# Sample rows of the input projection as fp32 products on 32-column tiles, and the stick-breaking sums of the prompt as rounded part and exact remainder

## The reference, cut to what matters

```python
def project(h, w_in, pos):
    B, T, _ = h.shape
    z = h @ w_in                       # h: 512 prompt rows, 8 sample rows; w_in: 1024 x 2840
    ...

def sb_attend(q, k, v, q_pos, k_pos):  # 8 heads of 64; for the prompt in blocks of 128 queries
    z = jnp.einsum('bqhd,bshd->bhqs', q, k) / math.sqrt(HEAD_DIM)
    mask = k_pos[None, :] < q_pos[:, None]
    log_1m = jnp.where(mask, jax.nn.log_sigmoid(-z), 0.0)
    after = lax.cumsum(log_1m, axis=3, reverse=True) - log_1m
    a = jnp.where(mask, jnp.exp(jax.nn.log_sigmoid(z) + after), 0.0)
    return jnp.einsum('bhqs,bshd->bqhd', a, v)
...
x = x + concat(rmsnorm(o_sb), rmsnorm(o_nsa)) @ w_out
x = x + square(relu(rmsnorm(x) @ w_up)) @ w_down
y = rmsnorm(x)
```

## Time and profile before

| | us |
|---|---|
| median of three runs | 1236.61 (1235.08 to 1242.04) |
| the profiled execution | 1237.38 |
| its span, first to last instruction | 1235.1 |
| PE busy | 1109.6 (90%) |
| PEld busy | 972.2 (79%) |
| DVE busy | 592.9 (48%) |
| ACT busy | 383.4 (31%) |
| POOL busy | 70.5 (6%) |

### The profile page before, as it was taken

One profiled execution on the slowest core, in us unless ns is written; L12 is line 12 of the kernel. 1 busy time (PEld: TensorE's weight loads), 2 busy tenths in 40 slices (PEclk: granted clock), 3 DMA queues, 4 the chain that ended last, 5 costly groups with the idle time before them and its releaser, 6 DMA issues.

```text
span 1235.1 us, 23204 instructions
## 1 busy us (share of the span) xinstructions
PE 1109.6 (90%) x8460; PEld 972.2 (79%) x8460; DVE 592.9 (48%) x991; ACT 383.4 (31%) x708; POOL 70.5 (6%) x83
## 2 busy tenths in 40 slices
PE   2999998789898997469999999999999999999993
PEld 2999898778788887335555566899999999998993
DVE  4221364667687863742134455544553234553332
ACT  4111212223333332126544455332222122231223
POOL 2000001111111100000000000010000000000002
PEclk9999998889899985559998999999999999999997
DMA  6428216999999932005567775222332322332221
GB/s 215 158 75 214 76 38 166 251 262 252 257 261 279 280 106 86 0 23 184 172 199 225 234 239 178 86 69 72 98 102 86 102 85 85 86 100 86 86 69 70
DMA packets 179085, 176.37 MB, mean 143 GB/s; under 512 B 13047, under 2 KB 139636, under 8 KB 176660
## 3 DMA queue, kind: packets, MB, share of 16 engines
q1 hardware_dynamic: 178610, 171.33, 49.2%
q10 hardware_dynamic: 418, 4.27, 1.1%
HBM read 169.67 MB, written 10.06 MB: 146 GB/s over the span
## 4 chain that ended last, share of the span: by engine, by line
PE 72%; SPq 10%; DVE 6%; issue 5%; DMA 4%; ACT 3%; POOL 0%; POOLq 0%; DVEq 0%; ACTq 0%
PE bank L605 67%; PE bank L609 5%; SPq L475 3%; SPq L514 3%; SPq L517 2%; DMA low_arena<-in_cache_nsa_slc_kv_dram 2%; SPq L468 1%; DMA high_arena<-in_state_nsa_win_kv_dram 1%; DMA high_arena<-in_x_sample_dram 1%; SPq L549 1%; ACT low_arena L1393 1%; SPq L544 0%; DMA high_arena<-in_w_in_dram 0%; DVE high_arena L1428 0%; POOL high_arena L1974 0%
## 5 line engine op out<-in xcount | busy, mean ns | idle before, releaser
L605 PE MATMUL bank<-high_arena 128*128 128x254 f32 (+8 forms) x1864 | 241.3, 346 | 8.8 <-ACT high_arena L1154 6.1
L605 PEld LDWEIGHTS bank<-high_arena 128*128 128x128 f32 (+4 forms) x1864 | 186.6, 153 | 49.6 <-issue 10.1
L609 PE MATMUL bank<-low_arena 128*128 128x128 f32 (+2 forms) x653 | 102.0, 299 | 36.1 <-DMA low_arena<-in_cache_nsa_slc_kv_dram 19.5
L1859 DVE TENSOR_TENSOR w_low<-high_arena,w_high 128x1024 fp32r<-128x1024 f32 x72 | 90.1, 1252 | 82.2 <-ACT w_high L1330 72.6
L605 PE MATMUL bank<-w_in_high,h_high 128*128 128x284 f32 (+1 forms) x400 | 119.2, 298 | 4.2 <-DVE low_arena L1482 2.6
L609 PEld LDWEIGHTS bank<-low_arena 128*128 128x128 f32 (+2 forms) x653 | 83.1, 159 | 47.4 <-issue 27.5
L605 PE MATMUL bank<-w_in_low,h_high 128*128 128x284 f32 (+1 forms) x400 | 118.6, 296 | 0.0
L605 PE MATMUL bank<-w_in_high,h_low_in 128*128 128x284 f32 (+1 forms) x400 | 118.5, 296 | 0.0
L1330 ACT ACTIVATE w_high<-high_arena 128x1024 fp32r<-128x1024 f32 x72 | 76.3, 1060 | 113.5 <-PE bank L605 112.5
L605 PE MATMUL bank<-a_high,w_high 128*128 128x256 f32 (+1 forms) x512 | 103.6, 283 | 5.3 <-issue 2.9
L605 PE MATMUL bank<-h_high,w_high 128*128 128x256 f32 (+1 forms) x512 | 103.7, 284 | 1.8 <-DVE h_low L1886 1.8
(11 more groups left out here) (205 smaller groups left out, 1540.4 us busy)
## 6 DMA issues: line engine op xcount, KB each, us to landing
low_arena<-in_cache_sb_kv_dram SPq DMA_DIRECT2D x128, 256.0 KB, 5.2
high_arena<-in_cache_sb_kv_dram SPq DMA_DIRECT2D x128, 256.0 KB, 3.6
high_arena<-in_cache_nsa_cmp_kv_dram SPq DMA_DIRECT2D x128, 128.0 KB, 5.5
high_arena<-in_w_up_dram SPq DMA_DIRECT2D x32, 512.0 KB, 4.0
high_arena<-in_w_down_dram SPq DMA_DIRECT2D x32, 512.0 KB, 3.7
high_arena<-in_w_in_dram SPq DMA_DIRECT2D x10, 1136.0 KB, 5.6
low_arena<-in_cache_nsa_slc_kv_dram SPq DMA_DIRECT2D x128, 64.0 KB
high_arena<-in_cache_nsa_slc_kv_dram SPq DMA_DIRECT2D x128, 64.0 KB, 3.0
```

The costliest lines, as they stand in the source:

```text
L605: return T.matmul(out, lhsT=l, rhs=r, start=start, stop=stop, **k)
L609: return T.transpose(out, in_, ident[0:n, 0:n])
L1859: V.tensor_tensor(w_lo_r[u], w_raw[u], w_hi[u], ALU.subtract).then_inc(sem(f"w_lo{u}"), 1)
```

## The change

It has two parts.

**Samples' projection.** The fifth row tile leaves the fp32r scheme. The samples' normed rows stay unsplit in a small tile `hs`, and for each block PE does 8 fp32 products (one for each k tile) with the raw `w_in` block as the moving operand and 8 columns of `hs` as the stationary one. Four of them go to column offsets 0, 32, 64, 96 of the array and bank rows 0, 32, 64, 96; the other four add to these. DVE then adds the four groups of 8 rows in a chain of one copy and three additions (`samples_out`). Since the remainder overwrites the raw block, the samples' products of block n+1 are done in the middle of block n, between row tiles 1 and 2, and `win_low(n+1)` waits for them. Block 0, whose remainder POOL writes early, is loaded a second time for them (`win_first`, from ACT's queue). The loops over blocks are written out.

**Stick-breaking sums.** DVE keeps the softplus values as rounded part (a copy) and remainder (a subtraction), and `sb_sum` multiplies each by `ntri` and `nones` (now rounded copies, made by two more ACT copies) as fp32r products. `sb_sum` moves in the step behind the samples' products and `sb_pv`.

```diff
             def z_rows(i, u, t):            # PE, row tiles 0 to 3: as before
+            def z_samples(raw):
+                for k in range(KD):
+                    c = 32 * (k % 4)
+                    ins = mm(bank[NT][c:c + B, 0:CB], hs[:, k, :], raw[:, k, :], k < 4, k >= 4, skip_group_check=True)
+                ins.then_inc(sem("z_mm"), 1)
+            def z_block(i, u, first=False, last=False):
+                pe.wait_ge(sem(f"w_lo{u}"), i + 1 + 1)
+                z_rows(i, u, 0)
+                if first:
+                    pe.wait_ge(sem("const_in"), 32)
+                    z_samples(win_first)
+                z_rows(i, u, 1)
+                if not last:
+                    pe.wait_ge(sem(f"win_in{1 - u}"), (i + u) * 16 + 16)
+                    pe.wait_ge(sem(f"z_ev{NT}"), i * 2 + (u + 2))
+                    z_samples(win[1 - u])
+                z_rows(i, u, 2)
+                z_rows(i, u, 3)
...
             def sb_sum(m):
-                pe.wait_ge(sem("sb_sp"), m + 1)
-                for h in range(2):
-                    ins = mm(out[:, 0:n], ntri, sp_tile(pr, i)[:, h], False, i == 3, skip_group_check=True)
-                    for j in range(3, i, -1):
-                        ins = mm(out[:, (j - i) * P:n], nones, sp_tile(pr, j)[:, h], False, j == i + 1, ...)
+                for low in range(2):
+                    pe.wait_ge(sem("sb_sp"), 2 * m + low + 1)
+                    for h in range(2):
+                        for j in range(i, NT):
+                            sp_ = (sp_low(pr, j) if low else sp_high(sums_hi_r, pr, j))[:, h]
+                            ...
+                            ins = mm(o, nones_r if j > i else ntri_r, sp_, False, low == 1 and j == NT - 1, ...)
...
-                if 1 <= s < SB_U + 1:
-                    sb_sum(s - 1)
                 for v in sample_steps(s):
                     sample_values(v)
...             # sb_pv(s - 2)
+                if 1 <= s < SB_U + 1:
+                    sb_sum(s - 1)
...
             win_high(0, 0)                  # ACT
+            act.dma_start(win_first, A["w_in"][0]...).then_inc(sem("const_in"), 16)
...
+            def win_low(n):                 # DVE
+                dve.wait_ge(sem(f"w_hi{n % 2}"), n // 2 + 1)
+                dve.wait_ge(sem("z_mm"), 5 * n - 1)
+                V.tensor_tensor(win_r[n % 2], win[n % 2], win_hi[n % 2], ALU.subtract).then_inc(sem(f"w_lo{n % 2}"), 1)
+            def z_block(n):
+                z_out(n, 0)
+                if n == 0:
+                    samples_out(0)
+                if n < NCB - 1:
+                    win_low(n + 1)
+                    samples_out(n + 1)
+                z_out(n, 2)
+                dve.wait_ge(sem("z_mm"), 5 * n + (5 if n == NCB - 1 else 6))
+                V.memset(st[0:1, 202:203], 0.0).then_inc(sem(f"win_free{n % 2}"), 1)
...
             def sb_soft(m):                 # DVE
-                V.scalar_tensor_tensor(out=sp_tile(pr, i), in0=bank_pair(...)..., op0=ALU.max, op1=ALU.add).then_inc(sem("sb_sp"), 1)
+                chain(V.scalar_tensor_tensor(out=v, in0=bank_pair(...)..., op0=ALU.max, op1=ALU.add))
+                V.tensor_copy(sp_high(sums_hi_r, pr, i), v).then_inc(sem("sb_sp"), 1)
+                V.tensor_tensor(low, v, high, ALU.subtract).then_inc(sem("sb_sp"), 1)
```

More of the change, by code:

```diff
@@ L293, in decoder_step @@
         win_hi, win_hi_r = zip(*(parts(f"w_in_high{u}", r.take(KD * CB), KD, CB) for u in range(2)))
+        win_first = view(r.take(KD * CB), KD, CB)
         r = Fields(r_at, TOTAL)
@@ L351, in decoder_step @@
         pbuf = view(late_at, 512)
-        spb = [z[:, NT, 0:2560].rearrange("p (h c) -> p h c", h=2), view(late_at, 2, 1280)]
+        z_r = rounded("z_parts", z_at, T5, COLS)
+        sums_hi_r = [z_r[:, NT, 0:2560].rearrange("p (h c) -> p h c", h=2), rounded("sums_high", late_at, 2, 1280)]
+        sums_hi = [s_.bitcast(F32) for s_ in sums_hi_r]
+        sums_lo_r = [[z_r[:, 0:2, O_QN:O_QN + 512], z_r[:, 2:4, O_QN:O_QN + 384], z_r[:, 0:2, O_C:O_C + 256], z_r[:, 2:4, O_C:O_C + P]],
+                     [rounded("sums_low0", osb_at + 4 * 512, 2, 512), rounded("sums_low1", osb_at + 6 * 512, 2, 384),
+                      z_r[:, 0:4, O_S:O_S + P].rearrange("p (h n) c -> p h n c", h=2), rounded("sums_low3", osb_at + 6 * 512 + 768, 2, P)]]
+        sums = view(r_at, 2, 512)
         w = Fields(late_at, TOTAL)
@@ L1099, in _ @@
             win_high(0, 0)
+            act.dma_start(win_first, A["w_in"][0].rearrange("(k p) c -> p k c", p=P)[:, :, (NCB - FIRST) * CB:(NCB - FIRST + 1) * CB]
+                          ).then_inc(sem("const_in"), 16)
             act.wait_ge(*signal("vcol_ev", 1))
@@ L1504, in rotary @@
                 dve.wait_ge(sem("rope_done"), t + 1)
[L1506 to L1517 removed]
+            for n in range(NCB):
+                if n >= FIRST:
+                    rotary(n - FIRST)
+                if n == NCB - 1:
                     rotary(NT)
[L1519 removed]
+                z_block(n)
             chain(V.memset(qbd[:, :, :], 0.0))
@@ L1766, in sb_soft @@
                     dve.wait_ge(sem("sb_c"), 4 * (pr - 1))
-                V.scalar_tensor_tensor(out=sp_tile(pr, i), in0=bank_pair(2 * (m % 3))[:, :, 0:n], scalar=0.0,
-                                       in1=ebuf[:, m % 2, :, 0:n], op0=ALU.max, op1=ALU.add).then_inc(sem("sb_sp"), 1)
+                v = sums[:, :, 0:n]
+                if m:
+                    dve.wait_ge(sem("sb_sp"), 2 * m)
+                chain(V.scalar_tensor_tensor(out=v, in0=bank_pair(2 * (m % 3))[:, :, 0:n], scalar=0.0,
+                                             in1=ebuf[:, m % 2, :, 0:n], op0=ALU.max, op1=ALU.add))
+                V.tensor_copy(sp_high(sums_hi_r, pr, i), v).then_inc(sem("sb_sp"), 1)
+                dve.wait_ge(sem("sb_sp"), 2 * m + 1)
+                low, high = sp_low(pr, i), sp_high(sums_hi, pr, i)
+                if len(low.shape) == 4:
+                    v, high = (a.rearrange("p h (n c) -> p h n c", c=P) for a in (v, high))
+                V.tensor_tensor(low, v, high, ALU.subtract).then_inc(sem("sb_sp"), 1)
             def sb_out(pr):
```

95 lines of the change are left out of this document (47 added, 48 removed).

## The result

| | before | after |
|---|---|---|
| median of the runs beside each other, us | 1239.32 (1235.08 to 1244.66, 4 runs) | 1223.21 (1222.58 to 1227.45, 4 runs) |
| ratio after / before | | 0.9875 [0.9826, 0.9924] |
| the profiled execution, its span, us | 1237.4, 1235.1 | 1223.6, 1221.7 |

What follows compares the result with a forecast made beforehand. PE was taken as the bound in both stages touched. Projection -13.7 and loop -12.8 us sum to -26.5: 1210.9 us for an execution like the profiled 1237.4, 1210.1 for the median, range 1200 to 1221.

Steps and rivals of the forecast that it cites:

- three new ones of 1.8: Attention loop: PE's present waits of about 1.4 us go, three new ones come: 0.1, 0.4 and 1.3 us.
- rival D: Loop: moved `sb_sum` uses up the one-step lag, each unit's chain runs bare, about 33 us a pair, 1273; chance 0.04.
- Rival A: Loop: each unit's remainder comes too late, DVE sets the pace, about 5 of 12.8 us left, 1218; chance 0.15.
- cancels: Projection: the clock falls after the late load's hole as it does now, 1.7 us, so no net cost.
- The products: Projection: 31.2 us of fifth-tile products go, samples' products at 1.08 us a block, 10.8 in all, come: -20.4 us.
- The late load: Projection, block 5: PE waits 8.1 us for block 6's `w_in` load where it waited 2.3, so +5.8 us.
- The margin of 0.4 us: Projection, other blocks: load there at 5.9 us, PE asks at 6.3; +1.0 us put for copies in flight and jitter.
- Sums, what goes and comes: Loop: fp32 sums of 9.25 us a pair become 5.6 as fp32r products, -14.6 us in four pairs.
- The small products, the disputed term: Loop sums: fp32r products of 128 columns take 0.066 to 0.14 us, 0.11 taken; the skill gives about 81 ns.
- Sums, the named waits: Loop: 1.3 us at the first NSA steps, +0.4 for mask copies on ACT, +1.0 for waits on pages.
- B: Projection: the late load does not hurt since the queue ahead runs faster; the 8.1 us vanish, 1202; chance 0.05.
- C: Projection: the four column offsets do not overlap, 3.9 us a block, total 1235, no change; chance 0.03.

Runs made afterwards that it cites:

- acc_first: Changed kernel with `acc_out` ahead of `sb_soft` in DVE's queue; 1213.43 us, 0.9821 of the kernel before, loop 76.5 us.
- acc_no_rest: `acc_first` without the remainder's products in `sb_sum` and PE's wait for them; 1204.69 us, 0.9732 of the kernel before, loop 68.7 us.
- queue_late: Changed kernel with compression weights and 16 cache loads issued behind all ten `w_in` loads; 1212.60 us, 0.9823 of the kernel before.
- proj_only: Changed projection with the sums of the kernel before; 1224.18 us, 0.9894 of the kernel before, loop 88.5 us.
- sum_first: Changed kernel with `sb_sum` back in its old place on PE, ahead of samples' products and `sb_pv`; 1219.96 us, 0.9881 of the kernel before.

## Why the prediction was wrong, step by step

**The step that failed** is "Following all 16 units in this way, I find the waits that PE has now ... gone, and three new ones of 1.8". What was followed were the units: scores, passes, softplus with its two new instructions, sums, values. The samples' work in between was counted as time that PE has to spend, and not as work that itself waits for DVE. `gather_values` waits for `acc_out`, and `acc_out` stands in DVE's queue behind the very instructions whose number the change raises. That wait takes 6.5 us in the loop, and the slow clock behind it 6.2, together 12.7 of the 13.9 us that `acc_first` brings back. In the prediction's sum the term "three new ones of 1.8" had to hold these 12.7 us and did not. With `acc_first`'s 9.8 us off, the median is 1213.4, inside the range.

The whole account, by the two profiles: the loop came out 14.7 us above its forecast (+1.9 against -12.8) and the projection 2.1 (-11.6 against -13.7). The unchanged stages came out 3.8 us below, which is luck. Together the span fell by 13.4 us instead of 26.5.

**The bound of a moved instruction.** The prediction weighed the move of `sb_sum` by the lag of its own unit (rival D) and by the cover of the remainder (rival A). It did not ask what `sb_sum` had been covering from its old place, and that was the gather, with 3.5 us to spare. Rival A gave 1218 for another reason; `acc_no_rest` shows that the remainder does not set the pace.

**The clock** was allowed for in the projection ("cancels") and not in the loop, since no hole was expected there. In the projection it nearly cancelled: the low clock cost 1.9 us behind the hole of 9.9 us (`queue_late`) and 1.7 behind the one of 2.3 us before. In the loop it cost 3.4 and 2.8 us, and no term held them.

**Projection, -13.7 forecast, -11.6 measured.** The products: a block of 13.84 us against 13.7, with 1.26 us for the samples against 1.08; in ten blocks 1.8 us too little. The extra time stands on both sides of the piece: its first product starts 0.22 us behind the last full one (67.33 to 67.55), and the second full product behind it 0.24 after the first (68.62 to 68.86), where full products start 0.13 apart. The Trainium skill (TensorEngine Tiling, Key Properties) says that changing the tiling mode drains the engine, and gives no time for it. The prediction's estimate for such a drain on the way in and on the way out, 1.08 + 0.13 = 1.21, is near the 1.26 measured; no run here separates the drain from the rest. The late load: its issue at 108.82 (forecast 108.2), the wait in block 5 behind tile 1, with tiles 2 and 3 hiding both parts, all as worked out. But it landed after 10.2 us instead of 8.1, so the wait was 9.9 and not 8.1. The load before landed while 216 GB/s were moved, this one at 192; why was not tested. The prediction took one landing from one trace as fixed: in the profiles with the changed projection and the old queue the same wait is 8.5 (`acc_first`), 9.9, 10.0 (`acc_no_rest`), 10.1 (`proj_only`) and 11.1 us (`sum_first`). The margin of 0.4 us in the other blocks held, so the 1.0 us put there for jitter was not needed. DVE's chain for the samples was as forecast, 1.9 us:

```profile
71.52 0.43 DVE L1534 COPY low_arena<-bank 8x284 f32<-8x284 f32 x1
71.99 0.92 DVE L1536 TENSOR_TENSOR low_arena<-low_arena,bank 8x284 f32<-8x284 f32 x2
72.94 0.45 DVE L1537 TENSOR_TENSOR low_arena<-low_arena,bank 8x284 f32<-8x284 f32 x1
```

**Sums, what goes and comes**: 9.25 us a pair became 6.14 and not 5.6, so the sums gave 12.4 us and not 14.6. The small products, the disputed term, were sized right:

```profile
558.14 0.28 PE L621 MATMUL bank<-sums_high,ntri_r 128*128 128x128 f32 x1
558.26 0.39 PE L621 MATMUL bank<-sums_low,ntri_r 128*128 128x128 f32 x2
```
```profile
543.24 0.33 PE L621 MATMUL bank<-z_parts,ntri_r 128*128 128x256 f32 x1
543.41 0.22 PE L621 MATMUL bank<-z_parts,nones_r 128*128 128x128 f32 x1
543.47 0.33 PE L621 MATMUL bank<-z_parts,ntri_r 128*128 128x256 f32 x1
```

Two products of 128 columns in a row start 0.12 us apart (558.14 to 558.26). A 256 with a 128 takes 0.23, from 543.24 to 543.47, which is the 0.12 + 0.11 that was taken; the starts inside the pair are 0.17 and 0.06 apart, so how the 0.23 divides is not shown. The Trainium skill (TensorE: Matmul & The Clock Gate, Back-to-back issue gap) has about 81 ns for the sustained product of 128 columns; the trace's 0.12 us doesn't agree, and the measurement decides. What was too small is the edge of each run of sums: the four sizes take 2.69, 1.79, 1.07 and 0.59 us by the timeline of `acc_first` (548.23 to 550.92, 542.73 to 544.52, 538.45 to 539.52, 535.73 to 536.32), each 0.15 to 0.19 over its products (four groups of 0.63, 0.40, 0.23 and 0.11), where 0.1 was allowed for all four together.

**Sums, the named waits**: 1.11 us at the first NSA steps (forecast 1.3), the mask copies 3.7 - 3.3 = 0.4 (0.4), waits for pages below 2 us (1.0). DVE's copy of 1024 elements took 0.69 (0.78), its subtraction 1.23 (1.2). Right, and small beside what was left out.

**Direction and rivals.** Faster was given 0.93, and it is faster. B and D are refuted by the wait of 9.9 us and the loop of 90.4 us, C by the 1.14 us of the eight products, and A because PE has no wait for the remainder. None of the cases has a wait at an instruction that the change does not touch, and that is where it was.

**Slips in the sums.** A sixth on top of 216 GB/s is 252, not 255, and rival C's products come to 39 - 31.2 = +7.8 us, not +7. Neither moves the forecast.

## What to carry to other kernels

When work is taken off an engine or moved in its stream, list every instruction that stood behind it there, and for each what it waits for; the slack that the removed work gave them is part of its price. On the engine that gets new instructions, list what other engine's work stands behind them in its queue: a short release (here a copy and a memset of 0.9 us) belongs ahead of a long chain that it does not need. And price a new hole on TensorE at more than its length: here 6.5 us of holes in the loop cost 12.7, and 9.9 in the projection 11.8.

## What the runs showed of the hardware

- Holes of 2.0 and 4.5 us in TensorE's stream came with about 6.8 us each at a granted clock of 0.50, the lower of its two levels, behind the first and from the end of the second on; in windows of 19 us the mean was 0.83 and 0.82. The low clock cost 3.4 and 2.8 us there, and 1.9 behind the hole of 9.9 us in the projection. Sixteen records of samples' products took 1.47 us behind the longer hole and 0.84 where there was none.
- fp32r products of 128 columns in a row (558.14 to 558.26) started 0.12 us apart, as those of 256 do in the MLP (two from 900.01 to 900.25).
- A DVE copy from float32 to fp32r of 1024 elements took 0.69 us, the subtraction of the same size 1.23, nearly twice as long.
- The same load of 1136 KB behind the same 16 page loads landed 8.1 us after its issue in one kernel and 10.2 in the other, and PE's wait for it was 8.5 to 11.1 us in five profiles with the same code up to there.
